# Attention with gated probabilities and values as stationary weights, in a decoder layer on one NeuronCore

## The reference, cut to what matters

```python
# B=1, S=256 tokens, G=4 groups, R=4 heads per group, d_qk=96, d_v=64, all float32
# three branches per head: 15 compressed keys, 256 selected keys, 256 window keys
logits = einsum('bgrsd,bgnd->bgrsn', q, k) * SCALE + bias      # each branch
p = masked_softmax(logits, mask)                               # each branch
o = g[0] * (p_cmp @ v_cmp) + g[1] * (p_slc @ v_slc) + g[2] * (p_win @ v_win)
y_a = o.transpose(...).reshape(B, S, 1024) @ w_attn_out
```

## Time and profile before

| | us |
|---|---|
| median of 3 runs | 1219.2 |
| the 3 runs | 1200.63, 1219.2, 1225.37 |
| profiled execution, its time | 1195.33 |
| its span, first to last instruction | 1193.6 |
| PE, DVE, ACT, POOL busy | 1004.1, 728.4, 278.1, 324.7 |
| attention, first score matmul to first output projection | 110.5 |

### The profile page before, as it was taken

The page is one execution under the profiler, slowest core; times in us unless marked ns, Lnnn a source line. Parts: engine busy times, 40 slices in busy tenths (PEclk is TensorE's granted clock), DMA queues, the critical chain, the costliest instruction groups (busy, mean ns, idle before and its releaser), DMA issues.

```text
span 1193.6 us, 10994 instructions
## 1 busy us (share of the span) xinstructions
PE 1004.1 (84%) x3386; PEld 617.0 (52%) x3386; DVE 728.4 (61%) x1772; ACT 278.1 (23%) x731; POOL 324.7 (27%) x311
## 2 busy tenths in 40 slices
PE   5899999999999996969888777788777777778676
PEld 5688888787667763845453333333333332333222
DVE  6699895222646313465547676777677767666553
ACT  3111122231535202231212221222132212221211
POOL 0201000010000000224335644444544444445420
PEclk9899999999959998989998989988998989989998
DMA  9977648838000232498788999999999999999992
GB/s 370 403 302 227 245 159 319 298 96 186 1 1 2 92 137 88 155 423 327 303 335 331 425 422 423 423 423 424 422 422 424 423 421 424 422 424 422 422 425 121
DMA packets 62536, 361.37 MB, mean 303 GB/s; under 512 B 7275, under 2 KB 7915, under 8 KB 29452
## 3 DMA queue, kind: packets, MB, share of 16 engines
q0 software_dynamic: 42400, 290.47, 60.4%
q1 hardware_dynamic: 20076, 70.18, 16.7%
HBM read 359.05 MB, written 1.57 MB: 302 GB/s over the span
## 4 chain that ended last, share of the span: by engine, by line
PE 49%; DMA 36%; DVE 5%; ACT 3%; issue 2%; POOL 2%; SPq 2%; POOLq 0%; ACTq 0%; DVEq 0%
DMA arena<-in_peer_uv,idx 33%; PE pb L423 21%; PE pb L649 13%; PE pb L454 4%; PE pb L575 2%; DMA ring<-in_w_stream 2%; PE pb L547 2%; POOL qT L396 2%; DVE arena L1205 1%; PE pb L474 1%; DMA hT<-in_peer_uv,idx 1%; PE pb L558 1%; PE pb L571 1%; ACT sig L845 1%; PE pb L530 1%
## 5 line engine op out<-in xcount | busy, mean ns | idle before, releaser
L649 PE MATMUL pb<-arena,sig 128*128 128x512 f32 x444 | 222.9, 651 | 62.4 <-ACT sig L845 62.4
L396 POOL DMA_INDIRECT arena<-in_peer_uv,idx x111 | 127.1, 1145 | 263.9 <-PE pb L649 137.6
L423 PE MATMUL pb<-hT,ring 128*128 128x256 f32 x880 | 190.7, 379 | 1.2 <-ACT hT L801 0.7
L1205 DVE CUSTOM_DVE_ANT_0 arena<-arena,sig 128x1024 f32<-128x1024 f32 x111 | 135.0, 1227 | 90.5 <-DMA arena<-in_peer_uv,idx 90.1
L649 PEld LDWEIGHTS pb<-arena,sig 128*128 128x128 f32 x444 | 91.2, 210 | 185.4 <-issue 185.4
L423 PEld LDWEIGHTS pb<-hT,ring 128*128 128x128 f32 x880 | 167.0, 190 | 25.2 <-ACT arena L708 1.7
L649 PE MATMUL pb<-ring,sig 128*128 128x512 f32 x208 | 110.0, 689 | 37.0 <-ACT sig L845 37.0
L840 ACT ACTIVATE gl<-dot 128x4 f32<-128x4 f32 x64 | 13.1, 205 | 407.7 <-DVE dot L1205 407.6
L649 PEld LDWEIGHTS pb<-ring,sig 128*128 128x128 f32 x208 | 45.0, 222 | 101.9 <-issue 101.9
L947 DVE SCALAR_TENSOR_TENSOR y<-arena,cols,y x240 | 95.2, 483 | 0.0
L845 ACT ACTIVATE sig<-ident,cf 128x128 f32<-128x128 f32 x256 | 81.8, 390 | 18.3 <-DVE cf L1211 18.3
(11 more groups left out here) (221 smaller groups left out, 1335.7 us busy)
## 6 DMA issues: line engine op xcount, KB each, us to landing
ring<-in_w_stream SPq DMA_DIRECT2D x103, 512.0 KB, 4.7
arena<-in_w_ada POOLq DMA_DIRECT2D x32, 512.0 KB, 9.9
arena<-in_w_ada SPq DMA_DIRECT2D x12, 512.0 KB, 13.1
arena<-in_w1k SPq DMA_DIRECT2D x8, 512.0 KB, 6.0
sig<-in_w_ada SPq DMA_DIRECT2D x4, 512.0 KB, 15.2
arena<-in_w1v POOLq DMA_DIRECT2D x1, 2048.0 KB, 8.1
arena<-rev_scratch POOLq DMA_DIRECT2D x8, 256.0 KB, 11.0
arena<-in_peer_uv,idx POOLq DMA_INDIRECT x111, 25.8
```

The source lines that it names most:

```text
L396: nc.gpsimd.indirect_dma_start(out=rowat[PLACE[n]], out_offset=None, in_=a["peer_uv"], in_offset=bass.IndirectOffsetOnAxis(ap=idx[:, c, e: ...
L423: last = mm(pb[:, bank, 0:SEQ], w[:, k * P:(k + 1) * P], src[:, k, :], start=(k == 0), stop=(k == DT - 1))
L649: last = mm(pb[:, 4 + 2 * t + hf, :], diag[:, c % DEEP, e, :], rowat[PLACE[n]][:, D + hf * 512:D + (hf + 1) * 512], start=(i == 0 and e == ...
L1205: V_.tensor_tensor_reduce(out=u, in0=u, in1=h2[:, c // CPT, :], scale=1.0, scalar=0.0, op0=ALU.mult, op1=ALU.add, accum_out=dot[:, c % DEE ...
```

## The change: what it does

- **Scores.** For the first tile the score matmul takes 128 keys of each branch, 256 columns in place of 512.
- **Gates before the values.** DVE no longer combines the results of the values. It computes reciprocal and gate share of each unit (`shares`), and multiplies the exponentials by them in place (`gated`, two instructions a unit), before they are transposed. The compressed probabilities are treated alike, once per group (`cmp_gated`).
- **Values.** The values are the stationary operand (64 columns) and the probabilities of all four heads of a group move through (512 columns). All branches and key blocks sum in one PSUM bank: 3 matmuls per group of the first tile, 5 of the second. They are issued once per group, at iteration n with n % 4 = 2, for the group that began six units before.
- **Result.** It comes out with the channels on partitions, and ACT copies it to `hT` in two instructions per group (`attention_out`); `attn`, its 16 transposes and their copies are gone.
- **Order.** Transposes come two iterations behind the scores, not one. `S` has four buffers and lies in `y`, `PT` and `PcT` hold a whole group and have two buffers. On DVE the order in an iteration is logits(n), shares(n-1), maxima(n), gated(n-1), and then the work on the compressed keys, which came first before.

```diff
@@ -180,22 +180,20 @@
 
 
         kcA, kcB, vcAB = (sc[:, 1024 * i:1024 * i + 1024] for i in range(3))
-        attn = xs
         ssb = sc[:, :].rearrange("p (t m k) -> p t m k", t=TT, k=NK)
         pair = sb("pair", [P, 2 * D])
         S_ = pair[:, 0:D]
-        S = S_.rearrange("p (u b t) -> p u b t", u=2, b=2)
+        S = yf.rearrange("p (u b t) -> p u b t", u=4, b=2)
         revsb = pair[0:HEADS, 0:512]
         wide = S_.rearrange("p (j t) -> p j t", j=DT)
         junk = sc[:, 0:1024]
         tmp = pair[:, D:2 * D]
-        PT = tmp.rearrange("p (a b) -> p a b", a=2)
+        PT = arena[:, 8:12, :].rearrange("p a b -> p (a b)").rearrange("p (u k t) -> p u k t", u=2, t=512)
         scaled = [tmp, sc[:, 1024:2048]]
         spare = sb("spare", [P, 2 * D])
-        PcT = spare[:, 0:512]
+        PcT = spare[:, 1024:2048].rearrange("p (u t) -> p u t", u=2)
         htok = spare[0:NCG, 0:512].rearrange("p (u n) -> p u n", u=2)
         tbc = spare[:, 512:512 + TT * HEADS * NCMP].rearrange("p (t h n) -> p t h n", t=TT, h=HEADS)
-        otmp = spare[:, 1024:1024 + 2 * 6 * DV].rearrange("p (a n) -> p a n", a=2)
 
         rowat = [arena[:, 2 * i:2 * i + 2, :].rearrange("p a b -> p (a b)") for i in range(6)]
         rowat += [hT[:, :, :].rearrange("p a b -> p (a b)"), pair[:, :], spare[:, :]]
...
@@ -543,68 +544,54 @@
                 tt, h, g, hh, keys = unit_keys(n)
                 if n >= 2:
                     pe.wait_ge(v_st, n - 1)
-
-                mm(pb[:, n % 2, :], qT[0:DQK, h, tt * P:(tt + 1) * P], kT[0:DQK, g, 1:3, :],
+                mm(pb[:, n % 2, 0:2 * keys], qT[0:DQK, h, tt * P:(tt + 1) * P], kT[0:DQK, g, 1:3, 0:keys],
                    start=True, stop=True).then_inc(p_s, 1)
 
             def transposes(n):
                 tt, h, g, hh, keys = unit_keys(n)
-                pe.wait_ge(a_exp, 2 * (n + 1))
+                pe.wait_ge(v_p, 2 * (n + 1))
                 if n >= 2:
                     pe.wait_ge(a_pt, n - 1)
                 for b in range(2):
                     for kb in range(tt + 1):
                         o = (b * (tt + 1) + kb) * P
-                        last = nc.tensor.transpose(pb[:, 2 + n % 2, o:o + P], S[:, n % 2, b, kb * P:(kb + 1) * P],
+                        last = nc.tensor.transpose(pb[:, 2 + n % 2, o:o + P], S[:, n % 4, b, kb * P:(kb + 1) * P],
                                                    ident[:, :])
                 last.then_inc(p_t, 1)
 
-            def values(n):
-                tt, h, g, hh, keys = unit_keys(n)
-                gi = n // REP
-                pe.wait_ge(a_pt, n + 1)
+            def values(gi):
+                tt, g = group_of(gi)
                 pe.wait_ge(a_pct, gi + 1)
-                if gi >= 1 and hh % 2 == 0:
-                    pe.wait_ge(v_o, 2 * (gi - 1) + hh // 2 + 1)
-                o = (hh % 2) * 3 * DV
-                bank = 6 + hh // 2
-                mm(pb[:, bank, o:o + DV], PcT[0:NCMP, hh * P:(hh + 1) * P], vcv[:, g * DV:(g + 1) * DV],
-                   start=True, stop=True)
+                pe.wait_ge(a_pt, REP * (gi + 1))
+                if gi >= 2:
+                    pe.wait_ge(a_o, 2 * (gi - 1))
+                o = pb[0:DV, 6 + gi % 2, :]
+                mm(o, vcv[:, g * DV:(g + 1) * DV], PcT[0:NCMP, gi % 2, :], start=True, stop=False)
                 for b in range(2):
                     for kb in range(tt + 1):
-                        last = mm(pb[:, bank, o + (1 + b) * DV:o + (2 + b) * DV],
-                                  PT[:, n % 2, (b * (tt + 1) + kb) * P:(b * (tt + 1) + kb + 1) * P],
-                                  V[:, kb, (b * GROUPS + g) * DV:(b * GROUPS + g + 1) * DV],
-                                  start=(kb == 0), stop=(kb == tt))
+                        last = mm(o, V[:, kb, (b * GROUPS + g) * DV:(b * GROUPS + g + 1) * DV],
+                                  PT[:, gi % 2, b * (tt + 1) + kb, :], start=False, stop=(b == 1 and kb == tt))
                 last.then_inc(p_o, 1)
 
-            for n in range(NU + 2):
+            for n in range(NU + 3):
                 if n < NU:
                     if n % REP == 0:
                         cmp_scores(n // REP)
                     scores(n)
-                    if n % REP == 1:
+                    if n % REP == 2:
                         cmp_transposes(n // REP)
-                if 1 <= n <= NU:
-                    transposes(n - 1)
-                if n >= 2:
-                    values(n - 2)
-
-
-            pe.wait_ge(v_at, 2 * GROUPS * TT)
+                if 2 <= n < NU + 2:
+                    transposes(n - 2)
+                if n >= REP + 2 and (n - 3) % REP == REP - 1:
+                    values((n - 3) // REP)
+
+
             pe.wait_ge(a_pt, NU)
             pe.wait_ge(a_pct, GROUPS * TT)
-            for t in range(TT):
-                for jj in range(2):
-                    for j in range(4):
-                        last = nc.tensor.transpose(pb[:, 2 + 2 * t + jj, j * P:(j + 1) * P],
-                                                   attn[:, t, (4 * jj + j) * P:(4 * jj + j + 1) * P], ident[:, :])
-                    last.then_inc(p_at, 1)
 
             wide_bank = (0, 1, 6, 7)
 
-            pe.wait_ge(a_xT, 4)
-            pe.wait_ge(v_o, 2 * GROUPS * TT)
+            pe.wait_ge(a_o, 2 * GROUPS * TT)
             for j in range(DT):
                 if j >= 4:
                     pe.wait_ge(v_m, j - 3)
...
@@ -767,39 +754,44 @@
 
             def exps(n):
                 tt, h, g, hh, keys = unit_keys(n)
+                act.wait_ge(v_mx, n + 1)
+                for b in range(2):
+                    fn(S[:, n % 4, b, 0:keys], S[:, n % 4, b, 0:keys], ACT.Exp, bias=nm[:, n % 2, b:b + 1],
+                       accum_out=Z[:, n % 2, b:b + 1]).then_inc(a_exp, 1)
+
+            def probabilities_out(n):
+                tt, h, g, hh, keys = unit_keys(n)
                 gi = n // REP
-                act.wait_ge(v_mx, n + 1)
+                act.wait_ge(p_t, n + 1)
                 if gi >= 2 and hh == 0:
-                    act.wait_ge(v_coef, 2 * (gi - 1))
-                for b in range(2):
-                    fn(S[:, n % 2, b, 0:keys], S[:, n % 2, b, 0:keys], ACT.Exp, bias=nm[:, n % 2, b:b + 1],
-                       accum_out=Z[:, gi % 2, hh, 1 + b:2 + b]).then_inc(a_exp, 1)
-
-            for n in range(NU + 1):
+                    act.wait_ge(p_o, gi - 1)
+                fn(PT[:, gi % 2, 0:2 * (tt + 1), hh * P:(hh + 1) * P],
+                   pb[:, 2 + n % 2, 0:2 * P * (tt + 1)].rearrange("p (k t) -> p k t", t=P), ACT.Copy).then_inc(a_pt, 1)
+
+            def attention_out(gi):
+                tt, g = group_of(gi)
+                act.wait_ge(p_o, gi + 1)
+                o = pb[0:DV, 6 + gi % 2, :].rearrange("p (a b t) -> p a b t", b=2, t=P)
+                for odd in range(2):
+                    fn(hT[odd * DV:(odd + 1) * DV, 2 * g:2 * g + 2, tt * P:(tt + 1) * P], o[:, :, odd, :],
+                       ACT.Copy).then_inc(a_o, 1)
+
+            for n in range(NU + 4):
                 gi = n // REP
                 if n < NU:
+                    exps(n)
                     if n % REP == 0:
                         act.wait_ge(v_csub, gi + 1)
                         fn(Sc[:, :, :], Sc[:, :, :], ACT.Exp).then_inc(a_cexp, 1)
-                    exps(n)
-                if n >= 1:
-                    u = n - 1
-                    tt = group_of(u // REP)[0]
-                    act.wait_ge(p_t, u + 1)
-                    if u >= 2:
-                        act.wait_ge(p_o, u - 1)
-                    fn(PT[:, u % 2, 0:2 * P * (tt + 1)], pb[:, 2 + u % 2, 0:2 * P * (tt + 1)],
-                       ACT.Copy).then_inc(a_pt, 1)
-                if n < NU and n % REP == 1:
+                if 2 <= n < NU + 2:
+                    probabilities_out(n - 2)
+                if n < NU and n % REP == 3:
                     act.wait_ge(p_ct, gi + 1)
-                    if gi >= 1:
-                        act.wait_ge(p_o, gi * REP)
-                    fn(PcT[0:NCMP, :], pb[0:NCMP, 5, :], ACT.Copy).then_inc(a_pct, 1)
-            for t in range(TT):
-                for jj in range(2):
-                    act.wait_ge(p_at, 2 * t + jj + 1)
-                    fn(hT[:, 4 * jj:4 * jj + 4, t * P:(t + 1) * P],
-                       pb[:, 2 + 2 * t + jj, :].rearrange("p (j t) -> p j t", j=4), ACT.Copy).then_inc(a_xT, 1)
+                    if gi >= 2:
+                        act.wait_ge(p_o, gi - 1)
+                    fn(PcT[0:NCMP, gi % 2, :], pb[0:NCMP, 5, :], ACT.Copy).then_inc(a_pct, 1)
+                if n >= REP + 3 and (n - 4) % REP == REP - 1:
+                    attention_out((n - 4) // REP)
 
             def row(v):
                 act.wait_ge(p_row, v + 1)
...
@@ -1025,51 +1017,55 @@
             def logits(n):
                 tt, h, g, hh, keys = unit_keys(n)
                 dve.wait_ge(p_s, n + 1)
-                if n >= 2:
```

(108 more changed lines are left out.)

## The result

The changed kernel takes 1229.7 us (median of 4 runs, 1227.1 to 1230.4). The kernel before, with one more run beside it, has a median of 1211.0. The ratio is 1.024, 95% interval 1.019 to 1.029: **slower by 2.4%**, where no change that can be told was forecast. All ratios here compare fast executions alone, which leaves out those of a kernel that took over 1.5% more than its shortest (the kernel before has such ones), so they aren't the quotients of the medians. By the medians the kernel is 18.7 us, 1.5%, slower.

What follows compares the result with a forecast made beforehand. PE bound attention before; afterwards PE and DVE taking turns would, at 103.4 us full clock. Slow stretches made it +6 us on the median of 1219.2: 1225, own range 1212 to 1240, wider 1202 to 1248.

Steps and rivals of the forecast that it cites:

- the loop: In attention, PE and DVE take turns once per group: 10.2 us in the first tile, 14.4 in the second.
- the small prices: Single operations in attention: gate multiplies 0.25 and 0.33 us, burst matmuls 0.86 us, at most 0.93.
- the clock: PE's clock in attention: at least one half-speed stretch again, 27 us at half clock costing +10 us.
- one or two slow stretches, +3 to +13: The main forecast for attention, chance 0.56: half-clock stretches put it +3 to +13 us, middle +6.
- the 103.4 us of full clock: Length of changed attention with no fall of the clock, summed from its loops and ends, against 96.9 before.
- a pure gain of 6.9 us: PE's work in the first tile: half-width scores save 0.43 us on each of 16 matmuls.
- Rival 2: Attention's clock stays low, from PE's 2 us idle ahead of compressed transposes: +24 us or more, up to +49; chance 0.19.
- The sum: Whole kernel: +6 us on the profiled run's 1195.3, giving 1201, all of it from attention.
- Rest of the kernel: 0: Outside attention: no change in time, as later stages move by as much as attention's end.
- the forecast's own signs of being wrong: Second-tile groups under 12.8 us apart at full clock, DVE not waiting there, or stages behind attention changing length.
- The full-clock worth of attention before: The kernel before's attention without its half-speed stretch: 110.5 - 13.6 = 96.9 us.
- The absolute time: Whole kernel: the same +6 us added to the earlier runs' median of 1219.2, giving 1225.

Runs made afterwards that it cites:

- e6: The changed kernel plus 35 overwritten 512-column matmuls on PE, ahead of its waits for three transposes in four and for compressed transposes: 1208.4 us, ratio 1.004.
- e3: The changed kernel with scores issued one iteration ahead, before the compressed transposes, transposes and values: 1207.8 us, ratio 1.004 against the kernel before.
- e5: The changed kernel with scores issued one iteration ahead and each group's value burst cut into pieces: 1185.2 us, ratio 0.986 against the kernel before.
- e1: The changed kernel with the 512-column score matmuls put back for the first tile: 1224.6 us, ratio 1.023 against the kernel before.
- e2: The kernel before with half-width scores in the first tile as its only change: 1218.2 us, ratio 1.016.
- e9: The kernel before with half-width scores and an overwritten 256-column matmul ahead of each of the first tile's 16 score matmuls: 1201.4 us, ratio 1.003.

## Why the prediction was wrong, by its own steps

**Right: the loop.** The wait that was forecast is there, once per group, with the engines and the lines named: DVE's logits wait for the scores behind the burst, PE waits about 2 us for the compressed gates. With the clock kept at 1.00 (e6) the loops are 11.3 and 15.6 us including fillers. No run shows them without fillers at full clock, but an estimate can be had from the changed kernel, the length of a loop times its mean clock, as if each low microsecond cost half of one: 16.2, 19.2 and 17.4 us for three loops of the second tile at 0.89, 0.73 and 0.80 (the third is 394.88 to 412.25) give 14.4, 14.0 and 13.9, against 14.4. One of the first tile, from compressed transposes to compressed transposes, gives 13.52 x 0.75 = 10.1, against 10.2:

```profile
394.88:412.25 17.37, 14.77 (x44) 5.56 (x44) 8.87 (x31) 7.54 (x24) 0.00 (x0) 0.80 0.00 1
321.69:335.21 13.52, 10.54 (x35) 4.60 (x35) 6.75 (x32) 5.83 (x24) 0.00 (x0) 0.75 0.01 2
```

e3 and e5 show that this wait, and no sum of work, is what to remove.

**Right: the small prices.** Gate multiplies were 0.278 and 0.345 against 0.25 and 0.33; their difference, 0.067 us for 128 elements, is 0.52 ns per element, the double rate that was argued. The burst's matmuls took 1.00 for the first and 3.58/4 = 0.90 for the others at full clock against 0.86, within the 0.93 that bounded it but for the first.

**The step that failed: the clock.** The forecast said "one or two slow stretches, +3 to +13", 27 to 40 us at 0.50. Measured were 69 us. The loss against the 103.4 us of full clock was 132.9 - 103.4 = 29.5 us, 0.43 per low microsecond, where the forecast's 10 for 27 is 0.37. The 103.4 is itself a forecast, so the 0.43 is an estimate. By it the price of a low microsecond was nearly right, and their number was off by a factor of almost two. The mistake was to carry over the pattern of the kernel before, one long stretch, to a kernel in which PE works in another rhythm. There the windows show eight low stretches, one for each burst. Six begin in PE's idle ahead of the compressed transposes or the last burst, two (368.88 and 403.01) up to 2 us after that idle has ended, and they end in the later part of the burst or up to 1.3 us behind it. The idle isn't all of it: in the first tile the narrower scores go with most of the low time (e1), and a clock that stays low on a PE that doesn't idle (e2) was in no rival. The forecast booked the narrower scores as a pure gain of 6.9 us.

**Rival 2's mechanism happened, and its threshold was wrong.** It had the place (the idle ahead of the compressed transposes) and the mechanism, with a chance of 0.19. It was said to decide at 0.7 of the stage at 0.50. A loss of +22.5 came with 0.52, because low stretches are not spread evenly over a loop: about 43 of the 68 us of the eight lines above fall on the bursts, which the path goes through. The argument against it, that PE at half clock is busy throughout and the clock comes back, was true (it comes back in each loop) and beside the point. The Trainium skill (TensorE: Matmul & The Clock Gate, "Why this matters for your kernels") warns of idle gaps between bursts of matmuls, but of longer ones than these. Its warning gave this rival no weight here, and the measurement decides: with idle of about 2 us in each group the clock fell in all eight.

**The sum.** Prediction: +6. Measured between profiled runs: +22.5 in attention, +1.7 ahead, +7.3 behind. "Rest of the kernel: 0" thus missed too, and a change of the stages behind attention was one of the forecast's own signs of being wrong. But the 7.3 can't be ascribed to the change. All ten experiments have stages behind attention of 796 to 800 us, among them e2 and e9, which are the kernel before but for their scores (797.4 and 796.0), against 791.6 in the profiled run of before, which was among that kernel's shorter executions. What makes up this difference stays open. The full-clock worth of attention before, 96.9, left out a second low stretch, from 397.47 to 400.88; with it, it is 95.2.

**The absolute time.** 1225 was forecast and 1229.7 measured, inside the range. That is luck: the median of 1219.2 that the sum was put on was 8 us above the 1211.0 of four runs, and the change of +6 was 13 below the +18.7 between the medians.

## What to carry to other kernels

When values or any other work are gathered into one burst on an in-order engine, look at what its partner needs from behind the burst, and issue that first; here the order alone was worth 22 us, and with the burst in pieces 44, in part through the clock. When a change makes TensorE wait in front of a long piece of work, work out the time with that piece at half clock too, not only the stage at its mean. And if taking columns from TensorE doesn't pay, look at the granted clock before looking for another wait: dummy matmuls in the idle time are a cheap test of it.
